# Hybrid encoder trunk, one core: head norms applied as scales of the residual additions, gate moved ahead of the last additions, own PSUM banks for the dense stage's first chunk, cw cleared later

## What is computed

```python
for i in range(DEPTH):                       # DEPTH = 2, 256 tokens, 1024 features
    h = rmsnorm(x, g_mix[i])
    u, q, k, v = jnp.split(h @ w_in[i], splits, axis=-1)
    y_ssm = ssm_mixer(u, ...)                # scan both ways, GELU, GLU, rmsnorm over 512
    y_att = diff_attention(q, k, v, ...)     # 4 heads of 128; rmsnorm over each head
    x = x + jnp.concatenate([y_ssm, y_att], axis=-1) @ w_out[i]
    h = rmsnorm(x, g_ffn[i])
    if i % 2 == 0:
        x = x + swiglu(h, w_gate, w_up, w_down)          # dense, 2752 wide
    else:
        x = x + moe_swiglu(h, ...)                       # top 2 of 8 experts, 3584 wide
return rmsnorm(x, g_final)
```

## Time and profile before

| | us |
|---|---|
| median of 3 runs | 1409.65 (1409.48 to 1409.79) |
| the profiled execution | 1415.03 |
| its span | 1413.2 |

### The profile page before, as it was taken

The page is one execution under the profiler, slowest core; times in us unless marked ns, Lnnn a source line. Parts: engine busy times, 40 slices in busy tenths (PEclk is TensorE's granted clock), DMA queues, the critical chain, the costliest instruction groups (busy, mean ns, idle before and its releaser), DMA issues.

```text
span 1413.2 us, 18998 instructions
## 1 busy us (share of the span) xinstructions
PE 1337.4 (95%) x7246; PEld 966.2 (68%) x7246; DVE 835.7 (59%) x1091; ACT 678.3 (48%) x997; POOL 139.7 (10%) x113
## 2 busy tenths in 40 slices
PE   6997989999799888999999999999999999999996
PEld 5865568888687656767676766667676566666763
DVE  6867554554396865565555665555655555655552
ACT  7467354443364842444455444445444444445442
POOL 1466000000025720000000000000000000000000
PEclk9999999999899997999999999999999999999999
DMA  7541335554533255799999999999999999999994
GB/s 303 173 182 41 122 150 190 196 178 156 201 90 120 97 189 220 274 421 389 409 421 421 422 420 419 411 420 421 420 421 419 411 421 420 422 421 421 421 422 165
DMA packets 66328, 432.43 MB, mean 306 GB/s; under 512 B 8192, under 2 KB 14720, under 8 KB 16832
## 3 DMA queue, kind: packets, MB, share of 16 engines
q1 hardware_dynamic: 64848, 426.45, 75.1%
q0 software_dynamic: 1392, 4.78, 1.0%
HBM read 425.96 MB, written 2.10 MB: 303 GB/s over the span
## 4 chain that ended last, share of the span: by engine, by line
PE 77%; DMA 9%; ACT 6%; DVE 5%; SPq 2%; issue 1%; ACTq 0%; DVEq 0%
PE ps L2272 19%; PE ps L2307 11%; PE ps L2258 9%; PE ps L2161 8%; PE ps L2289 6%; PE ps L1925 5%; PE ps L2140 4%; DMA raw<-wmoe 4%; DMA first_ring<-wmoe 4%; PE ps L2066 2%; PE ps L2043 2%; PE ps L2081 2%; SPq L578 2%; DMA cst<-consts 1%; PE ps L1966 1%; PE ps L2054 1%
## 5 line engine op out<-in xcount | busy, mean ns | idle before, releaser
L2161 PE MATMUL ps<-wsplit,xh 128*128 128x512 f32 (+1 forms) x352 | 113.5, 394 | 4.9 <-DVE hv L1452 3.3
L1462 DVE TENSOR_TENSOR low_raw<-raw,last_uppers 128x2048 fp32r<-128x2048 f32 x39 | 89.1, 2290 | 37.9 <-ACT last_uppers L885 37.9
L1462 DVE TENSOR_TENSOR low_first<-first_ring,first_uppers 128x2048 fp32r<-128x2048 f32 x31 | 70.8, 2291 | 37.1 <-ACT first_uppers L885 37.1
L2307 PE MATMUL ps<-raw,hn 128*64 128x256 f32 x784 | 92.4, 382 | 0.0
L1925 PE MATMUL ps<-hT,mixw 128*128 128x256 f32 x384 | 88.6, 393 | 2.6 <-DMA mixw<-wmix 1.6
L1462 DVE TENSOR_TENSOR low_raw<-raw,first_uppers 128x2048 fp32r<-128x2048 f32 x31 | 70.8, 2290 | 32.4 <-ACT first_uppers L885 32.4
L1426 DVE TENSOR_TENSOR wsplit<-raw,wsplit 128x2048 fp32r<-128x2048 f32 x33 | 74.5, 2289 | 20.0 <-ACT wsplit L844 20.0
L1730 DVE TENSOR_TENSOR hv<-hv,ps 128x256 f32<-128x256 f32 x56 | 23.6, 422 | 105.5 <-ACT hv L1046 105.5
L1925 PEld LDWEIGHTS ps<-hT,mixw 128*128 128x128 f32 x384 | 75.0, 197 | 14.5 <-issue 2.0
L2307 PE MATMUL ps<-last_ring,hn 128*64 128x256 f32 x704 | 83.2, 382 | 0.0
L1046 ACT ACTIVATE hv<-ps 128x256 f32<-128x256 f32 x56 | 21.5, 384 | 127.4 <-PE ps L2272 127.4
(11 more groups left out here) (365 smaller groups left out, 2900.1 us busy)
## 6 DMA issues: line engine op xcount, KB each, us to landing
raw<-wmoe SPq DMA_DIRECT2D x148, 1024.0 KB, 22.5
first_ring<-wmoe SPq DMA_DIRECT2D x95, 1024.0 KB, 23.4
last_ring<-wmoe SPq DMA_DIRECT2D x91, 1024.0 KB, 23.0
raw<-wdense SPq DMA_DIRECT2D x33, 1024.0 KB, 5.2
mixw<-wmix SPq DMA_DIRECT2D x12, 2048.0 KB, 8.8
cyt<-bmat SPq DMA_DIRECT2D x2, 2048.0 KB, 11.9
qk<-wglu SPq DMA_DIRECT2D x2, 1024.0 KB, 5.1
X<-x_in SPq DMA_DIRECT2D x2, 512.0 KB, 5.5
```

The source lines that it names most:

```text
L1462: tt(lows[at], ring[at], uppers[k % UPPERS].bitcast(F32), ALU.subtract).then_inc(s["lo_done"], 1)
L2161: ins = mm(to, x2[:, fx, t * P:(t + 1) * P], of, start=(fx == 0 and i == 0), stop=(fx == KT - 1 and i == 2))
L2307: ins = mm(to, xlight[:, m % 2, fx], of[:, :, q * P:(q + 1) * P], start=(fx == 0), stop=(fx == KT - 1), tile_position=(0, LCAP * q))
```

## The change

- `oms` becomes four matmuls of one column, one for each row block and head, so that the sum of squares of a token lies on its partition. ScalarE's root and VectorE's reciprocal work on 128x4 (`head_inverse`).
- cat is no longer scaled. Each head has its own unit: 8 units `atn` of one matmul for a pair, in place of 4 of two, all in the step of the pair (4) and the next (4). They wait for `head` and for a bank. VectorE's addition takes the head's factor as a scale and alone waits for it.
- The last four additions of the second pair stand behind the two halves of the gate, two behind each. The splits of the first two weight pieces (`lower` 0 and 1, or `split` A0 and B0 in layer 1) stand behind these.
- In the dense stage the first chunk accumulates gate and up in banks 2 and 3, and the third piece does not wait for hv_ready. The first row block of the first piece takes its matmuls with xh first and those with xl last. ScalarE squares the second row block of X after the copies to xh. VectorE makes the first product before the sixth split.
- At the start of layer 1 VectorE takes the root of row block 0, adds the second half of the dense output, and then scales row block 0. The clearing of ush stands behind the scaling, the tags at the end of the steps (step 16). GpSimd clears cw after both row blocks are scaled (hn_ready) and not when the dense stage ends.

```diff
         if 0 <= i - ATN_AT[b] < 2:
-            work += [(f"atn{b}.{2 * (i - ATN_AT[b]) + k}", "D") for k in range(2)]
+            work += [(f"atn{b}.{4 * (i - ATN_AT[b]) + j}", "D") for j in range(4)]
...
+        def dense_bank(j, t):
+            return 2 + t if j < 2 else t
...
                 if l:
-                    pool.wait_ge(s["piece_done"], 3 * NC_D)
+                    pool.wait_ge(s["hn_ready"], TT * (l + 1))
                 nc.gpsimd.memset(cw[:], 0.0).then_inc(s["cw_zero"], 1)
...
-                                ins = nc.scalar.activation(hv[:, t], ps[:, t, 0:HC], ACT.Silu, scale=col[:, 6 + t:7 + t])
+                                ins = nc.scalar.activation(hv[:, t], ps[:, dense_bank(j, t), 0:HC], ACT.Silu,
+                                                           scale=col[:, 6 + t:7 + t])
...
-                        nc.scalar.activation(osq[:, b], ps[:, bank(u)].rearrange("p (a t) -> p a t", a=2), ACT.Sqrt,
+                        nc.scalar.activation(col[:, 96 + 4 * b:100 + 4 * b], ps[:, bank(u), 0:4], ACT.Sqrt,
                                              bias=col[:, 18:19], scale=1.0 / (2 * HD)).then_inc(s["emptied_act"], 1)
...
-                ffn_squares(l)
+                ffn_square(l, 0)
+                if l:
+                    ffn_square(l, 1).then_inc(s["fsumsq"], 1)
                 if l == 0:
                     for k in range(4):
...
                         ins.then_inc(s["xh_part"], 1)
+                    ffn_square(l, 1).then_inc(s["fsumsq"], 1)
                     act.wait_ge(s["xl_part"], 4)
...
-            def norm_scale(m):
-
-                for t in range(TT):
-                    dve.wait_ge(s["sumsq"], TT * m + t + 1)
-                    ts(col[:, 4 + t:5 + t], col[:, 2 * t:2 * t + 1], 1.0 / D, EPS, ALU.mult, ALU.add).then_inc(s["rstd"], 1)
-                    small_act()
-                    link(nc.vector.reciprocal(col[:, 6 + t:7 + t], col[:, 8 + t:9 + t]))
-                    ts(hn[:, t], X[:, t], col[:, 6 + t:7 + t], None, ALU.mult).then_inc(s["hn_ready"], 1)
+            def dense_out(t):
+
+                if t == 0:
+                    dve.wait_ge(s["dense_half"], 1)
+                else:
+                    dve.wait_ge(s["piece_done"], 3 * NC_D)
+                xs = X[:, t].rearrange("p (a n) -> p a n", a=2)
+                tt(xs, xs, ps[:, 2 + 2 * t:4 + 2 * t], ALU.add).then_inc(s["dense_added"], 1)
...
-            def head_norm(l, b):
+            def head_inverse(l, b):
 
                 dve.wait_ge(s["emptied_act"], emptied(unit(l, f"oms{b}"))[1])
-                heads = cat[:, FT + 2 * b:FT + 2 * b + 2]
-                link(nc.vector.reciprocal(osq[:, b], osq[:, b]))
-                tt(heads, heads, osq[:, b], ALU.mult).then_inc(s["normed"], 1)
-
-            def attention_out(l, b, at):
-
-                for k in range(2 * at, 2 * at + 2):
-                    u = unit(l, f"atn{b}.{k}")
+                c = slice(96 + 4 * b, 100 + 4 * b)
+                nc.vector.reciprocal(col[:, c], col[:, c]).then_inc(s["inverse_ready"], 1)
+
+            def attention_out(l, b, units):
+
+                dve.wait_ge(s["inverse_ready"], HEADS // 2 * l + b + 1)
+                for j in units:
+                    t, a, n = j // 4, j // 2 % 2, j % 2
+                    u = unit(l, f"atn{b}.{j}")
                     full(u)
-                    if b:
-                        dve.wait_ge(s["emptied_dve"], emptied(unit(l, f"atn{b - 1}.{k}"))[1])
-                    xs = X[:, k // 2, (k % 2) * 512:(k % 2) * 512 + 512]
-                    tt(xs, xs, ps[:, bank(u)], ALU.add).then_inc(s["emptied_dve"], 1)
+                    if a:
+                        dve.wait_ge(s["emptied_dve"], emptied(unit(l, f"atn{b}.{j - 2}"))[1])
+                    elif b:
+                        dve.wait_ge(s["emptied_dve"], emptied(unit(l, f"atn{b - 1}.{j + 2}"))[1])
+                    c = 96 + 4 * b + 2 * t + a
+                    xs = X[:, t, n * 512:(n + 1) * 512]
+                    stt(xs, ps[:, bank(u)], col[:, c:c + 1], xs, ALU.mult, ALU.add).then_inc(s["emptied_dve"], 1)
...
-                    if more or not isinstance(g, int) or j + RING * g + AHEAD < 3 * stack.n:
+                    first = nt == TT and j == 1
+                    ahead = more or not isinstance(g, int) or j + RING * g + AHEAD < 3 * stack.n
+                    if ahead and not first:
                         lower(stack, j + AHEAD, g)
...
                         ins.then_inc(s["hv_ready"], 1)
+                    if ahead and first:
+                        lower(stack, j + AHEAD, g)
...
-                if l:
-                    dve.wait_ge(s["in_exact"], 32)
-                    rows_at = distr.bitcast(F32).rearrange("p (a t) -> p a t", a=TT)[:, :, 0:1]
-                    for light in range(2):
-                        nc.vector.tensor_copy(tags[:, light, :, 0:1], rows_at)
-                        ins = ts(tags[:, light, :, 1:2], rows_at, -1.0, None, ALU.add)
-                    ins.then_inc(s["rows_tagged"], 1)
+                for t in range(TT):
+                    norm_root(l, t)
+                    if l and t == 0:
+                        dense_out(1)
+                    norm_rows(l, t)
                 nc.vector.memset(ush[:, :, 0:NCH + 1:NCH], 0.0).then_inc(s["u_zero"], 1)
-                norm_scale(l)
...
                     for f in range(2 * k, 2 * k + 2):
                         ins = ts(cat[:, f], yt[:, f], par[:, l, Q_GSSM + f:Q_GSSM + f + 1], None, ALU.mult)
                     ins.then_inc(s["cat_ready"], 1)
+                    attention_out(l, 1, range(4 + 2 * k, 6 + 2 * k))
...
                 ins.then_inc(s["qs_ready"], 1)
+                if l == 0:
+                    lower(stack, 0, 0)
+                    lower(stack, 1, 0)
+                else:
+                    split("A", 0)
+                    split("B", 0)
...
-                    ins = mm(ps[:, bank(u)], ones, osq[:, h], start=True, stop=True)
+                    for t in range(TT):
+                        for a in range(2):
+                            at = 2 * t + a
+                            ins = mm(ps[:, bank(u), at:at + 1], osq[:, h, a, t * P:(t + 1) * P], ones[:, 0:1],
+                                     start=True, stop=True)
...
-                    pe.wait_ge(s["normed"], HEADS // 2 * l + h + 1)
-                    for a in range(2):
-                        f = FT + 2 * h + a
-                        ins = mm(ps[:, bank(u), :], cat[:, f, t * P:(t + 1) * P], mixw[:, c % 2, f, :],
-                                 start=(a == 0), stop=(a == 1))
+                    empty_wait(unit(l, f"head{2 * h + a}"))
+                    ins = mm(ps[:, bank(u), :], cat[:, f, t * P:(t + 1) * P], mixw[:, c % 2, f, :], start=True, stop=True)
...
-                        at_least(pe, "hv_ready", k if nt == TT else k - 1)
+                        if nt < TT or j != 2 or not isinstance(g, int) or g:
+                            at_least(pe, "hv_ready", k if nt == TT else k - 1)
...
-                        b = t if nt == TT else c % 2
+                        b = dense_bank(j, t) if nt == TT else c % 2
+                        if nt == TT and j == 0 and t == 0:
+
+                            for x2, w2, ready in ((xh, wh, "xh_part"), (xh, wl, "xh_part"), (xl, wh, "xl_part")):
+                                for f in range(4):
+                                    if f % 2 == 0:
+                                        pe.wait_ge(s[ready], f // 2 + 1)
+                                    ins = mm(ps[:, b], x2[:, f, 0:P], w2[slot][:, f * 512:(f + 1) * 512],
+                                             start=(x2 is xh and w2 is wh and f == 0), stop=False)
+                            continue
```

More of the change, by code:

```diff
@@ L1484, in _ @@
                 for i in range(STEPS):
[L1485 to L1491 removed]
+                    if l and i == GP:
+                        dve.wait_ge(s["in_exact"], 32)
+                        rows_at = distr.bitcast(F32).rearrange("p (a t) -> p a t", a=TT)[:, :, 0:1]
+                        for light in range(2):
+                            nc.vector.tensor_copy(tags[:, light, :, 0:1], rows_at)
+                            ins = ts(tags[:, light, :, 1:2], rows_at, -1.0, None, ALU.add)
+                        ins.then_inc(s["rows_tagged"], 1)
                     if i < GP:
@@ L1551, in _ @@
                     stream(stack, TT, False)
[L1552 to L1559 removed]
+                    dense_out(0)
+                    dve.wait_ge(s["dense_added"], 1)
             dve.wait_ge(s["gain_in"], 16)
```

52 lines of the change are left out of this document (23 added, 29 removed).

## The result

The changed kernel takes **1394.93 us** (median of 3 runs, 1393.73 to 1395.99) against 1409.65 us before: ratio 0.9895, 95% interval 0.9873 to 0.9918. It is faster by 14.7 us. The prediction was 1385.8 us, in a range of 1381.5 to 1392.5: the direction holds, and the median is 9.1 us above the forecast and 2.4 us above the range. From profile to profile the gain is larger, 1415.03 to 1393.73 us, 21.3 where 23.9 were predicted. That the two differences do not agree is the subject of what follows.

The account below looks back on a forecast made before the run. TensorE was taken as the bound, busy 95% of the span, with the expert stage's weight stream nearly full too. Gains 14.2 + 1.3 + 6.1 + 2.3 = 23.9 us gave 1391.1 profiled, less 5.4: 1385.8 us, range 1381.5 to 1392.5.

Parts of the forecast that it names:

- The median of the runs is 5.4 us below the profiled one: Whole kernel: the forecast profile time of 1391.1 us, lowered by this same difference, becomes a median of 1385.8 us.
- Part 1: End of each layer's mixer: waits for scaled heads and gate go, 7.1 us a layer, 14.2 us for two.
- 2.0 + 1.7: Mixer's output projection: the wait for the gated output and the low clock behind it go, 3.7 us a layer.
- 136.0 instead of 139.06: 3.1 us: Layer 0's mixer: the last state-space outputs (L1986) start earlier because the projections wait for no norm.
- low clock in new places: Sign, anywhere in the new profile, that the forecast is wrong; no size given.
- Part 2: Dense stage: earlier start 1.3 us; the third piece's 3.3 us wait and 2.8 us of low clock go, 6.1 us.
- Part 3: Transition into layer 1: the stall behind GpSimd's clearing of cw goes, 2.3 us, between 0 and 4.1.
- Rival (a): Start of layer 1: clearing cw blocks VectorE's evictions of hT, Part 3 worth 0, total 21.6, 1388.0 us; chance 8%.
- (b): Dense stage: third piece's low half comes late, gap stays, total 18 to 20 us, about 1391 us; chance 6%.
- (d): Attention part of the mixers: VectorE's 32 additions pace TensorE, slower than before, 1414 us; chance 2%.
- (c): Expert stage: shorter layer 1 mixer squeezes weight loads, costing at most 7 of the 24 us, 1393 us; chance 6%.
- The sum: Whole kernel: 14.2 + 1.3 + 6.1 + 2.3 = 23.9 us gained.

Follow-up runs that it names:

- 9.5 alone: Kernel before with only the scaling of heads at the addition, the gate ahead of the last additions and the first splits behind it: 1399.48 us, ratio 0.9920.
- the third execution of before: Kernel before, unchanged, profiled a third time: 1409.77 us, 5.3 us shorter than the 1415.03 us execution used for the prediction.
- the heads alone: Kernel before with the heads scaled at the addition and nothing else, run twice: 1408.24 us (ratio 0.9991), then 1407.09 us (0.9970).
- the kernel with part 2 alone: Kernel before with only the dense-stage edits (own banks for first chunk, no wait for first product, high halves first): 1404.42 us, ratio 0.9958.
- the filled kernels: Kernels with identity transpositions in TensorE's waits: kernel before 1401.81 us, with heads scaled at the addition 1398.69, changed kernel 1387.69, then 1386.42.
- the clock held high: Kernel before and changed kernel, both with identity transpositions in TensorE's waits: 1401.81 us (ratio 0.9930) and 1386.42 us (0.9831).
- the filled kernel before: Kernel before with identity transpositions in TensorE's waits, including those for scaled heads, gate and first dense product: 1401.81 us, ratio 0.9930.
- the filled heads: Kernel before with heads scaled at the addition and identity transpositions in TensorE's waits, less the 18 ahead of the scaled heads: 1398.69 us, ratio 0.9914.

## Why the prediction went wrong, point by point

**"The median of the runs is 5.4 us below the profiled one ... I take the same difference off it."** This step failed first: without it the number is 1391.1 us, 2.6 under the changed kernel's profile and 3.8 under its median. The 5.4 us were not an overhead of profiling. The profile above that is 5.3 us shorter gains 4.6 of them ahead of the routing, where its low clock costs 4.4 us less; so they were mostly stretches of low clock that this one execution of before had and that one had not. The 9.6 us of low clock priced in the sum contain two of these stretches already (3.4 us, in layer 1), so that much was taken off twice.

**Part 1, 14.2 us.** Measured 9.5 alone. The mechanism is right as to the waits: they are gone, L1986's successor needs only GpSimd's last sum, and the additions keep up. All 32 of the changed kernel (ns min/median/max, first and last start):

```profile
L1440 DVE SCALAR_TENSOR_TENSOR X<-ps,col,X x32: 744/751/752, 135.2 to 510.4; 128x512 f32<-128x512 f32 x32
```

The terms "2.0 + 1.7" and "136.0 instead of 139.06: 3.1 us" were mis-sized. The second holds 1.7 us too, since L2043 took 5.37 us there instead of 3.67. In layer 1 of two of three executions of before there is nothing of either 1.7. Free of them the heads give 1.9 us a layer: from the third turn to the GLU's products (L2054 and its successors) layer 1 takes 22.3 us in the third execution of before, 20.4 in both of the heads alone. That makes 3.8 for two, and 1.7, 4.1 and 3.1 were measured.

The gate gives 2.0 a layer by its wait, and 8 us for two where it was taken back from the changed kernel; with 3 to 13 us inside the intervals the runs do not tell what its low clock adds. The profiles tell more: the eight unfilled ones that have the wait for the gate have it 16 times, and 12 times TensorE's next eight passes take 5.4 us, in the other four 3.7. So the 1.7 us behind the gate are there in most executions and not in all. What the price left out is that low clock can come elsewhere when these waits are gone. In layer 0 of the profiled execution it took 3.0 us ahead of the place, nearly as much as the 3.4 us that went behind the heads and the gate there; the prediction had named low clock in new places as a sign that it was wrong.

**Part 2, 1.3 + 6.1 us.** In the profiles 1.2 and 6.2, as priced, by the expected steps: no idle time between the second and third piece. In the runs 4.5 together. The wait of 3.3 and its 2.8 of low clock are not the same in every execution: two of the three profiles of before have them, in the other the wait is 1.93 us and the stretch lies ahead of it, at 183 to 186.

**Part 3, 2.3 us.** Measured 2.7 in the profiles, 2.0 in the runs. Rival (a) is refuted. L1226 takes 1.73 us inside the clearing of cw, as in the earlier trace rows and as it does with the clearing already over (1.73 us in the kernel with part 2 alone). So these tensor_scalars with their source in PSUM are not held. The Trainium skill (page "SBUF — State Buffer", section "Who interferes with whom") says only that tensor_scalar can contend, when its operands meet the conditions of the mode that uses both ports. The prediction left this condition out when it said that by the list alone the part would give nothing. The other page of the Trainium skill that it named, "VectorE: DVE Perf Modes" (section "Why PSUM operands drop a tier"), excludes PSUM from that mode, and the 1.73 us agree. And what the clearing held before the change were five small instructions for 2.0 to 2.3 us, not seven.

**Rivals (b) and (d)** did not come, and (c) is not shown. There is no gap in the dense stage; the additions do not pace TensorE. The expert stage is 1.7 us longer in the changed kernel's profile, but over all eighteen profiles of this case, of kernels with and without the change, it runs from 845.4 to 848.9 us. The kernel before has 845.4 to 847.9 in three, the changed one 847.6 and 848.4 in two, and of the filled kernels the changed one is the shorter (845.5 for 846.1): a price of the shorter mixer is not shown, and one of about 1 us is not excluded.

**The sum.** Of the 23.9 us, 9.6 were low clock (2 x 1.7 for the heads, 2 x 1.7 for the gate, 2.8 in the dense stage). Without them it is 14.3; measured were 14.7, then 14.8 by the medians and 16.5 by the ratio, and 15.4 with the clock held high, where only waits count. The intervals of 0.3 to 0.5% leave some 4 to 7 us of room around each number, so the agreement by itself is weak. The low clock itself can be compared: it costs 20.6 us in the mean of the three profiles of before (23.6, 19.9, 18.2) and 15.8 in the mean of the two of the changed kernel (17.4, 14.1). So 4.8 us of it went where 9.6 were priced: the other half is the term that was mis-sized. The mean granted clock over whole runs says the same, 0.982 in the 20 runs of before and 0.985 in the six of the changed kernel. The two accounts do not close to the microsecond: ahead of the router's prefix sums the changed kernel is 18.5 us shorter in the mean of these profiles, and 1.3 of it are lost behind them, which is no more than the scatter there.

Low clock does cost (filling wins 9.4 us before the change and about 7 after), but it is not bound to these waits: take one away, and it can fall behind another, as in the four of twelve unfilled profiles of this case in which the turn of layer 0's third head is followed by 10 us of it. What stays open is what sets the length of a stretch.

## What to carry to other kernels

Price a wait at its own length. Add the low clock behind it only by the share of several profiled executions that show it, and ask which waits stay that it can fall behind instead: where a stretch falls differed between two executions of one kernel that came to it 2 us apart. Never correct a sum by the distance between one profiled execution and the median of the runs unless you know what that distance is made of. Where TensorE waits often for 1 to 2 us, matmuls that nobody reads, in the wait and no longer than it, into the bank that is overwritten next, are worth trying: the change with them, at 0.9840 and 0.9831 of before, beats both kernels. Filling a single wait moved the idle time to the next one; only filling the chain of them kept the clock.

## What was not expected of the hardware

A stretch at 1.2 GHz can outlast the idle time that it followed by far. In the profiled execution of the filled kernel before, a wait of 2.4 us that ends at 43.86 is followed by 20 us without a pause at 0.50:

```profile
43.86 2.08 PE L1960 MATMUL ps<-ush,bw 64*128 64x128 f32 x16 [2.38 <-ACT qk L943]
45.87 13.91 PE L1972 MATMUL ps<-cw,cyt 128*128 128x64 f32 x64
```

```profile
40.00:44.00 4.00, 1.62 (x9) 0.99 0.89 171
44.00:64.00 20.00, 20.00 (x101) 0.50 0.01 2
```

The 64 matmuls of L1972 take 13.91 us, and 7.36 (L1991) in the changed kernel's profile; so the work does run at half speed there. That execution took 1413.86 us, 11.5 more than any other of that kernel (1400.04 to 1402.34); the filled heads show the same stretch (0.57 over the 20 us) and their slowest run. At the same place the changed kernel waited 1.3 us and kept its clock. The mean granted clock of that execution is 0.986, of the other six of its kernel 0.993 to 0.996; 20 us at half clock are 10 us, or 0.007 of a run. The runs of the kernel before at 1417.8, 1420.0 and 1420.8 us have the lowest clock of all its runs, 0.974 to 0.975, where the others have 0.978 to 0.987. So such a stretch is a likely cause of them too; where it lay is not known, since none of them was profiled.
